# One block-diagonal 128x128 product for the rotary part of the page scores, in place of zero-padded column-tiled ones

## The reference

```python
def mla_sample_attend(qn, qr, c_kv, k_r, p, ckv_pool, kr_pool, page_table):
    ckv_past = ckv_pool[page_table].reshape(Bsz, -1, KV_RANK)    # 8 x 4096 x 256
    kr_past = kr_pool[page_table].reshape(Bsz, -1, B_ROPE)       # 8 x 4096 x 32
    q_lat = jnp.einsum('bthd,rhd->bthr', qn, p['w_uk'])
    s_past = (jnp.einsum('bthr,bsr->bhts', q_lat, ckv_past)
              + jnp.einsum('bthe,bse->bhts', qr, kr_past)) * ATTN_SCALE
    ...
    w = softmax over past and new positions
    o_lat = einsum(w, ckv_past) + ...
```

## Time and profile before

| what | value |
|---|---|
| median of three runs | 3512.46 us (3499.12 to 3525.58) |
| span of the profiled execution | 3545.2 us (the page gives no other time for it) |
| PE busy, weight loads busy | 3315.6 us (94%), 3061.3 us (86%) |
| DVE, ACT, POOL busy | 1331.5, 1096.7, 133.7 us |
| mean granted TensorE clock | 0.958 |
| the page stage of the two layers | 894 to 1110 us and 2638 to 2854 us |

### The profile page before, as it was taken

The page is one execution under the profiler, slowest core; times in us unless marked ns, Lnnn a source line. Parts: engine busy times, 40 slices in busy tenths (PEclk is TensorE's granted clock), DMA queues, the critical chain, the costliest instruction groups (busy, mean ns, idle before and its releaser), DMA issues.

```text
span 3545.2 us, 69005 instructions
## 1 busy us (share of the span) xinstructions
PE 3315.6 (94%) x27968; PEld 3061.3 (86%) x27968; DVE 1331.5 (38%) x1838; ACT 1096.7 (31%) x1595; POOL 133.7 (4%) x168
## 2 busy tenths in 40 slices
PE   8999999988888999999999999998988899899998
PEld 7999988767666998999999998986776689899997
DVE  3333344356222444333333334444642224433333
ACT  2222243144332324222232213332433323332213
POOL 0000000000221000000000000000012300000000
PEclk9999999699998999999999999998999999999998
DMA  5322231111542322322133222301034423222221
GB/s 133 90 86 80 71 79 33 33 30 49 188 168 92 89 86 66 89 87 82 57 96 89 86 80 54 96 16 50 26 101 176 175 59 95 65 81 85 86 84 55
DMA packets 443313, 296.31 MB, mean 84 GB/s; under 512 B 24328, under 2 KB 430572, under 8 KB 434986
## 3 DMA queue, kind: packets, MB, share of 16 engines
q1 hardware_dynamic: 430265, 217.05, 21.8%
q0 software_dynamic: 12928, 77.64, 5.9%
HBM read 286.44 MB, written 8.34 MB: 83 GB/s over the span
## 4 chain that ended last, share of the span: by engine, by line
PE 85%; ACT 5%; DVE 4%; another core or an unknown queue 4%; issue 2%; DMA 0%; DVEq 0%; SPq 0%; ACTq 0%
PE ps L619 64%; PE ps L966 3%; PE ps L1002 2%; PE ps L668 2%; PE ps L647 1%; PE ps L981 1%; PE ps L659 1%; PE ps L912 1%; ACT res L1200 1%; ACT x_hi L1199 1%; DVE ckv_t L1774 1%; PE ps L1016 1%; PE ps L903 1%; ACT prob L1365 1%
## 5 line engine op out<-in xcount | busy, mean ns | idle before, releaser
L1492 DVE TENSOR_TENSOR w_lo<-w_raw,w_hi 128x1024 fp32r<-128x1024 f32 x436 | 533.8, 1225 | 1082.9 <-ACT w_hi L1166 1082.9
L619 PE MATMUL ps<-x_hi,w_hi 128*128 128x268 f32 x4032 | 839.4, 289 | 34.0 <-DVE x_lo L1531 25.7
L1166 ACT ACTIVATE w_hi<-w_raw 128x1024 fp32r<-128x1024 f32 x436 | 460.7, 1057 | 1226.3 <-PE ps L619 1214.2
L619 PE MATMUL ps<-x_lo,w_hi 128*128 128x268 f32 x4032 | 829.6, 287 | 0.0
L619 PE MATMUL ps<-x_hi,w_lo 128*128 128x268 f32 x4032 | 828.2, 287 | 0.0
L619 PEld LDWEIGHTS ps<-x_hi,w_hi 128*128 128x128 f32 x4032 | 631.8, 189 | 42.6 <-DVE x_lo L1531 33.3
L619 PEld LDWEIGHTS ps<-x_lo,w_hi 128*128 128x128 f32 x4032 | 634.4, 189 | 0.0
L619 PEld LDWEIGHTS ps<-x_hi,w_lo 128*128 128x128 f32 x4032 | 631.3, 189 | 0.0
L619 PE MATMUL ps<-h_hi,w_hi 128*128 128x268 f32 x1408 | 294.6, 291 | 0.6 <-DVE w_lo L1492 0.3
L619 PE MATMUL ps<-h_hi,w_lo 128*128 128x268 f32 x1408 | 290.3, 288 | 0.0
L619 PE MATMUL ps<-h_lo,w_hi 128*128 128x268 f32 x1408 | 289.4, 287 | 0.0
(11 more groups left out here) (361 smaller groups left out, 3699.3 us busy)
## 6 DMA issues: line engine op xcount, KB each, us to landing
w_raw<-in_ffn_up SPq DMA_DIRECT2D x180, 512.0 KB, 3.8
w_raw<-in_w_in SPq DMA_DIRECT2D x72, 512.0 KB, 3.8
w_raw<-in_ffn_down SPq DMA_DIRECT2D x64, 512.0 KB, 3.7
w_raw<-in_ffn_down SPq DMA_DIRECT2D x32, 384.0 KB, 3.1
w_raw<-in_w_o SPq DMA_DIRECT2D x16, 512.0 KB, 3.7
c_smp<-in_state_C SPq DMA_DIRECT2D x16, 256.0 KB, 2.9
out_new_C_sample<-c_smp SPq DMA_DIRECT2D x16, 256.0 KB, 2.4
w_raw<-in_w_pa SPq DMA_DIRECT2D x16, 256.0 KB, 2.7
```

The costliest lines, as they stand in the source:

```text
L619: ins = mm(ps[0:m, 2 * p + half, 0:HT], w[:, s, off + t_ * m:off + t_ * m + m], x[part][:, k0 + t_, half * HT:(half + 1) * HT], start=firs ...
L1166: f(w_hi[:, s, :], w_raw[:, s, :], ACT.Copy).then_inc(hi_made, 1)
L1492: v.tensor_tensor(w_lo[:, s, :], w_raw[:, s, :], w_hi[:, s, :].bitcast(F32), ALU.subtract).then_inc(lo_made, 1)
```

## The change

In `score_q` the four rotary products of each quarter go. In quarters 0 and 2 one product is put ahead of the latent ones: the whole of `qz_cur` (128 rows, 4 x 32 = 128 columns, block-diagonal) as the stationary operand, `kr_t` of this quarter and the next (256 columns) as the moving one. It writes 256 columns of all 128 partitions of bank 6, so that the next quarter needs none of its own. It opens the bank's accumulation in quarter 0; the latent products now all accumulate onto it. The wait for `kr_read` moves behind the waits for `q_copied` and `u_exp`, to the product.

```diff
                     pe.wait_ge(pg_read_v, u4 + 1 + 2)
                     pe.wait_ge(pg_read_l, u4 + 1 + 2)
-                    if q % 2 == 0:
-                        pe.wait_ge(kr_read, l * 32 + i * 4 + h2 * 2 + q // 2 + 1)
                     if q == 0:
                         pe.wait_ge(q_copied, l * DEC + i + 1)
                         pe.wait_ge(u_exp, l * 16 + i * 2 + h2 + 1)
+                    if q % 2 == 0:
+                        pe.wait_ge(kr_read, l * 32 + i * 4 + h2 * 2 + q // 2 + 1)
+                        mm(ps[:, 6, q * P:(q + 2) * P], qz_cur[:, :, :], kr_t[:, q:q + 2, :], start=q == 0, stop=False, skip_group_check=True)
                     for r in range(2):
                         for j in range(4):
-                            mm(ps[32 * j:32 * j + 32, 6, q * P:(q + 1) * P], q_cur[:, r, :], ckv_t[:, q % 2, r, j * P:(j + 1) * P],
-                               start=r == 0, stop=False, skip_group_check=True)
-                    for j in range(4):
-                        ins = mm(ps[32 * j:32 * j + 32, 6, q * P:(q + 1) * P], qz_cur[:, j, :], kr_t[:, q, :], start=False, stop=True, skip_group_check=True)
+                            ins = mm(ps[32 * j:32 * j + 32, 6, q * P:(q + 1) * P], q_cur[:, r, :], ckv_t[:, q % 2, r, j * P:(j + 1) * P],
+                                     start=False, stop=r == 1, skip_group_check=True)
                     ins.then_inc(u_score, 1)
```

## The result

The changed kernel is slower: 3533.22 us, median of 16 runs (3507.59 to 3558.64), against 3507.47 us for the kernel before (16 runs, 3491.52 to 3537.71); ratio 1.0075, interval 1.0047 to 1.0102. A repeat of the same kernel in the experiments gave 1.0047 (1.0013 to 1.0080). Both intervals leave out 1: a small loss, within the 1% to which the prediction had given 0.83, but not the no change that was argued for. The forecast was 3511 us, the range 3480 to 3530; the result lies 3 us above it.

The account below looks back on a forecast made before the run. The prediction took TensorE, busy 94% of the span, as the bound, with a hold in 28 page-stage units. Terms -7.4, -0.8, -3.2 and +9.6 sum to -1.8 us on the runs' median 3512.5: 3511 us, range 3480 to 3530.

Parts of the forecast that it names:

- the hold of 3.8 us: Unnamed wait before quarter 3's copy delays `score_q` 3 in 28 units; each costs 2.65 us, together 74 us.
- a rival: The hold shrinks with fewer TensorE records: 18.6 us less, 3492 us, chance 0.16; wholly gone 74 us, 3437 us, 0.10.
- `score_q` 3 loses 0.23 us: Its rotary products go, with the unit's maximum, exponential, turn and values behind it: 32 units, -7.4 us.
- a free unit: Unit without the hold, four in all: `score_q` 1 and 2 changes give net -0.19 us each, -0.8 us.
- `score_q` 0, +9.6 us: Grows by 0.20 ahead of the values product, plus 0.10 for a weight load, in 32 units; ends +6.4 and +12.2.
- the load of 0.10: Exposed 128-column weight load of `score_q` 0's full product, between 0 and 0.19 us; 0.10 taken.
- The sum of the stream: TensorE's tiled products out, 29.4 us, full products in, 27.5 us: stream shrinks by 1.9 us.
- The clock falls: Rival: units with fewer instructions double the page stage's share at the lower clock, up to 15 us a layer: 3541 us, 0.04.
- a stage clock below 0.88: Sign that the forecast is wrong: page stage's mean granted clock under 0.88, against 0.93 in the profile.
- unnamed waits clearly below 3 us: Sign that the forecast is wrong: DVE's unnamed waits, expected again near 14 of 3.8 us a layer, become shorter.
- The drain: Rival: tiled records wait for the full product's end, 0.37 us more a product, 13 us in all: 3524 us, chance 0.08.
- -3.2: `score_q` 1's saving in the 28 held units, half of -6.4 us taken; ends 0 and -6.4.

Follow-up runs that it names:

- with the clock held: 14 idle products behind each unit's last scores, in both kernels: ratio 0.9979 for the changed kernel, 1.0003 for the kernel before.
- thin gathers: Gathers from the third unit on fetch rows of 1 KB and 128 B, not 8 KB and 1 KB: ratio 0.9884 for the kernel before, 0.9830 changed.
- before again: The kernel before, unchanged, run and traced a second time: ratio 1.0001, page stages 190.0 and 188.5 us.
- tiled ahead: The kernel before with its four tiled rotary products kept for each quarter but put ahead of the latent ones: ratio 0.9972.

## Why the prediction was wrong

- **What bounds the stage.** Here it failed first. The prediction took the hold of 3.8 us, 28 times (27 in the trace: 14 and 13 in the layers), as the state of the kernel, and units without it as the exception. No later trace has it. Without it the stages of the same kernel are 53.5 us shorter (378.5 against 432), not the 74 us that the prediction set for it; the wait for the gather comes in its place. The warning was in the table: a span of 3545.2 us, 20 above the highest of the three runs shown. The prediction named this, made it an argument in a rival, and carried on with the difference. Behind the hold, the loop through the gather couldn't be seen: in the first trace no wait of TensorE for the gather shows, since the gather had always landed by then.
- **"`score_q` 3 loses 0.23 us ... Nothing hides it: 32 x -0.23 = -7.4 us."** This step failed. The time after `score_q` 3 is the wait for the gather, which hid the saving and grew by it: 23.2 us became 28.5 in layer 0. The saving itself was sized well: 0.42 us from the second rotary transposes to the last score (4.77 to 4.35), which is the 0.23 of this step and the 0.19 of a free unit in the next one.
- **`score_q` 0, +9.6 us.** The place was right, the product's own time too: 0.43 us on the chain for L979, as worked out, in place of 0.22. But of the 0.30 us a unit only some 0.05 reaches the loop (4.44 to 4.49), and with the clock held the two stages differ by 1.0 us. The term that hides the rest is the wait for `p_t`, which the prediction named and left out; the load of 0.10 that was added doesn't show. (The upper end of this term, +12.2, should read 32 x 0.39 = 12.5.)
- **The sum of the stream.** 29.4 us out, 27.5 us in. Where TensorE is the bound, with thin gathers, this and the pieces of a free unit hold: 0.42 us saved from the second rotary transposes on, 0.19 added ahead of them (medians), and 5.5 us less in the stages.
- **"The clock falls": 3541 us, chance 0.04, "Nothing in the rows asks for it".** This is what happened. A clock of 0.98 means 4% of the stage at 1.2 GHz, one of 0.92 or 0.91 means 16 to 18%. The price was near the 3533 measured; the mechanism was missing: not fewer instructions, but a longer wait at the gather, in which what they saved piled up. The sign set for it, a stage clock below 0.88, was measured off the odd trace's 0.93 and so would have missed it at 0.91. The other sign, unnamed waits clearly below 3 us, did show: there were none.
- **The drain.** In the timeline of the changed kernel, a unit at 2.4 GHz:

```profile
971.91 0.60 PE L979 MATMUL ps<-kr_t,qz_cur 128*128 128x256 f32 x2
972.44 1.08 PE L982 MATMUL ps<-ckv_t,q_cur 128*32 128x128 f32 x32
```

  From start to start 0.53 us, of which two records stream 0.43, so 0.10 for the change of shape, as behind the transposes (0.08 by the earlier trace rows). The 0.37 us of the rival didn't come. The drain on a change of the tiling mode, in the Trainium skill (TensorEngine Tiling (Array Packing), Tiling Modes, Key Properties), agrees with this trace at about 0.1 us.

The forecast of 3511 us is within 4 us of the kernel before, 3507, because terms of -7.4, -0.8, -3.2 and +9.6 us nearly cancelled, none of which came to the time of the kernel at that size; that it lies only 0.6% off is luck. The 26 us from 3507 to 3533 are, but for a few, the clock.

## What to carry to other kernels

Before costing an edit, hold the profiled execution against the runs: if it is longer than all of them, its largest unexplained wait is a suspect, and not the ground to stand on. Where a stage goes round a loop through a DMA, ask of each piece whether it lies in the loop or beside it: time saved beside it turns into waiting, time added inside it is paid, as far as nothing there was waiting anyway, and moving work out of the loop is worth more than making it cheaper. And an engine that waits longer may come back at half the clock, so that saving work can cost time.

## What the runs showed of the hardware

A wait of about 2 us in a unit of 11.5 to 13.4 us was enough for TensorE's granted clock to fall from 2.4 to 1.2 GHz in many units (0.91 to 0.94 in the stage); with waits 0.4 us shorter and a little more work beside them it stayed at 0.98, and with the wait partly filled by idle products at 0.98 to 0.99. Unit by unit, in the traces of before again, the change, its repeat and tiled ahead (28 units each): after a wait for the gather under 1.8 us none of 55 units ran its transposes at the lower clock, after one of 1.8 to 2.0 us 12 of 29, after a longer one 26 of 28. The step is thus steep just here, and the kernel before, with 1.66 us a unit, stood close to its edge.

The first trace's hold, in which DVE's copies began some 3.8 us late on a release that the profile doesn't name, while a gather was in flight, was not seen again in 13 further traces, 11 of them with the same gathers.
